# Block inverses of the delta-rule lane: 16x16 diagonal blocks on GpSimd through DRAM, four chunks side by side, levels in kept columns only

## The reference, cut to what matters

```
h = x                                   # (512, 2048)
proj = h @ w_in                         # 4 x 1024 columns + 128 for the delta rule, 4 x 1024 for the gated one
# delta rule (RWKV-7), 16 heads of 64, state S (64 x 64) per head, over t:
sa = S @ a_t
S  = S * w_t + outer(sa, b_t) + outer(v_t, k_t)
o_t = S @ r_t
# gated linear attention (HGRN-2), 8 heads of 128, in chunks:
att[t,s] = (q_t * exp(b_t - b_s)) . k_s   for s <= t
y = concat(o_rwkv, o_hgrn) @ w_out ; h = layer_norm(alpha * x + y)
```

## Time and profile before

| | |
|---|---|
| median of 3 runs | 3407.63 us (3407.55 to 3409.55) |
| the profiled execution: its own time, its span | 3406.94 us, 3405.2 us |
| PE busy | 3214.7 us, 94% |
| VectorE, ScalarE busy | 1726.9 us (51%), 1216.3 us (36%) |
| GpSimd busy | 71.5 us (2%), DMA issues nearly all |
| third block on PE | from about 1680 us to the end |

### The profile page before, as it was taken

One profiled execution on the slowest core, in us unless ns is written; L12 is line 12 of the kernel. 1 busy time (PEld: TensorE's weight loads), 2 busy tenths in 40 slices (PEclk: granted clock), 3 DMA queues, 4 the chain that ended last, 5 costly groups with the idle time before them and its releaser, 6 DMA issues.

```text
span 3405.2 us, 41072 instructions
## 1 busy us (share of the span) xinstructions
PE 3214.7 (94%) x16498; PEld 2578.3 (76%) x16498; DVE 1726.9 (51%) x2865; ACT 1216.3 (36%) x2150; POOL 71.5 (2%) x132
## 2 busy tenths in 40 slices
PE   7999999999999999999999999898999898989896
PEld 5777777777778877777788787777777787877685
DVE  5444444444433355555533546465665555555544
ACT  4333333333323233433333334343434343434421
POOL 0000000000000000000000000000000000000200
PEclk9999999999999999999999999999999999999998
DMA  4222222222233322122243211121211111111532
GB/s 150 75 81 75 75 81 75 76 77 78 68 125 129 106 69 70 67 69 69 98 142 118 68 54 59 44 69 40 70 52 57 56 59 54 63 53 53 192 130 87
DMA packets 79915, 274.86 MB, mean 81 GB/s; under 512 B 9952, under 2 KB 10592, under 8 KB 78960
## 3 DMA queue, kind: packets, MB, share of 16 engines
q1 hardware_dynamic: 63936, 232.13, 20.2%
q0 software_dynamic: 15792, 40.11, 3.5%
HBM read 252.21 MB, written 19.92 MB: 80 GB/s over the span
## 4 chain that ended last, share of the span: by engine, by line
PE 82%; DVE 11%; ACT 3%; issue 3%; DMA 0%; SPq 0%; DVEq 0%; POOL 0%; ACTq 0%
PE bank L253 13%; PE bank L255 13%; PE bank L254 13%; PE bank L257 7%; PE bank L259 7%; PE bank L258 7%; PE bank L1145 2%; PE bank L1152 2%; PE bank L277 2%; PE bank L429 1%; PE bank L1213 1%; PE bank L1159 1%; DVE mc L1082 1%; PE bank L306 1%; PE bank L456 1%
## 5 line engine op out<-in xcount | busy, mean ns | idle before, releaser
L253 PE MATMUL bank<-ma_split,mc_split 128*128 128x512 f32 x2304 | 976.1, 424 | 39.2 <-DVE ma_split L805 18.8
L255 PE MATMUL bank<-ma_split,mc_split 128*128 128x512 f32 x2304 | 908.9, 394 | 0.0
L254 PE MATMUL bank<-ma_split,mc_split 128*128 128x512 f32 x2304 | 905.3, 393 | 0.0
L670 DVE TENSOR_TENSOR mc_split<-mc,mc_split 128x1024 fp32r<-128x1024 f32 x426 | 519.8, 1222 | 428.8 <-ACT mc_split L519 423.9
L519 ACT ACTIVATE mc_split<-mc 128x1024 fp32r<-128x1024 f32 x426 | 448.3, 1054 | 297.7 <-PE bank L257 252.9
L253 PEld LDWEIGHTS bank<-ma_split,mc_split 128*128 128x128 f32 x2304 | 438.3, 190 | 147.7 <-issue 51.8
L255 PEld LDWEIGHTS bank<-ma_split,mc_split 128*128 128x128 f32 x2304 | 435.7, 189 | 97.8
L254 PEld LDWEIGHTS bank<-ma_split,mc_split 128*128 128x128 f32 x2304 | 439.0, 191 | 71.0 <-issue 3.8
L1325 ACT ACTIVATE mc<-bank 128x512 f32<-128x512 f32 x192 | 114.6, 597 | 391.5 <-PE bank L1159 269.1
L528 ACT ACTIVATE mc<-bank,stat 128x128 f32<-128x128 f32 (+3 forms) x128 | 67.6, 528 | 511.4 <-DVE stat L678 511.1
L257 PE MATMUL bank<-mc_split,ma_split 128*128 128x512 f32 x576 | 230.2, 400 | 5.1 <-DMA ma_split<-y 5.0
(11 more groups left out here) (353 smaller groups left out, 4030.4 us busy)
## 6 DMA issues: line engine op xcount, KB each, us to landing
mc<-in_w SPq DMA_DIRECT2D x426, 512.0 KB, 3.2
x<-mc POOLq DMA_DIRECT2D x8, 1024.0 KB, 5.0
y<-mb_split POOLq DMA_DIRECT2D x28, 256.0 KB, 2.8
ma_split<-y POOLq DMA_DIRECT2D x28, 256.0 KB, 7.6
mb<-in_xt SPq DMA_DIRECT2D x8, 512.0 KB, 12.4
mc<-in_x POOLq DMA_DIRECT2D x4, 1024.0 KB, 6.3
mc<-x POOLq DMA_DIRECT2D x4, 1024.0 KB, 5.9
mb<-x POOLq DMA_DIRECT2D x4, 1024.0 KB, 9.8
```

What stands on the lines that cost most here:

```text
L253: mm = pe.matmul(banks[j][:], wh[:, c], act_hi[:, kt, :], start=(kt == 0), stop=False)
L254: pe.matmul(banks[j][:], wl[:, c], act_hi[:, kt, :], start=False, stop=False)
L255: last = pe.matmul(banks[j][:], wh[:, c], act_lo[:, kt, :], start=False, stop=(kt == KT - 1))
L670: dve.tensor_tensor(w_low[:, s % NR, :, :], w_raw[:, s % NR, :, :], w_high[:, s % NH, :, :].bitcast(F32), ALU.subtract).then_inc(w_lo, 1)
```

## The change

1. `m8`, `xt`, `xw` hold eight matrices (two heads, four chunks), so a unit goes through the chunk part once, in 24 steps. `xw` takes the place of `xx` and `wsb`. Room is made by NH = 3 high buffers in place of 4.
2. The 16x16 diagonal blocks of all eight inverses (64 blocks) are made by GpSimd: `m8` is stored to DRAM, its diagonal blocks are loaded with one block on each of 64 partitions, 15 steps of a multiply and an add make the inverses, they are stored, and the 128x128 matrices that hold them are loaded back into `xt`. PE waits for that load (`xt_in`) ahead of its first X.
3. Only levels 4, 5 and 6 are left on PE, VectorE and ScalarE. A W or T matmul has 64 moving columns (those that the level keeps) in place of 128, and so has the copy behind it; the seven levels of the gated branch too.
4. Steps stand further apart: the four G steps (step 9 to 12 of the unit) every 3 points, then 37 points between the last G and the first X, levels every 3 points, the steps behind them every 2.5.

```diff
-NR, NH, LEAD = 5, 4, 2
+NR, NH, LEAD = 5, 3, 2
...
-                if k < 59:
-                    return 120 * u + 28 + 2 * (k - 9)
-                return 120 * u + 128 + 3 * (k - 59)
+                begin = 120 * u + 28
+                i = k - 9
+                if i < 4:
+                    return begin + 3 * i
+                if i < 13:
+                    return begin + 46 + 3 * (i - 4)
+                if i < CHUNK_K:
+                    return begin + 73 + 5 * (i - 13) // 2
+                return begin + 102 + 3 * (i - CHUNK_K)
...
+            def halves(x, lv):
+                v = x.rearrange("p q (n x t) -> p q n x t", x=2, t=1 << lv)
+                return v[:, :, :, 0, :], v[:, :, :, 1, :]
...
+                elif i < 13:
+                    lv, part = FIRST_LEVEL + (i - 4) // 3, (i - 4) % 3
+                    for p in range(2):
+                        mats = range(4 * p, 4 * p + 4)
+                        if part == 0:
+                            if lv == FIRST_LEVEL:
+                                pe.wait_ge(xt_in, 16 * (u + 1))
...
+                            for q in mats:
+                                mm = pe.transpose(C_BANK[f"X{lv}{p}"][:, q % 4 * P:(q % 4 + 1) * P], xt[:, q, :], ident[:])
+                        elif part == 1:
+                            c_wait(pe, "act", u, f"X{lv}{p}")
+                            to = halves(four(C_BANK[f"W{lv}{p}"][:]), lv)[0]
+                            for q in mats:
+                                mm = pe.matmul(to[:, q % 4], m8[:, q, 0:P], halves(xw, lv)[0][:, q], start=True, stop=True)
...
+            def sub_inverses(pool, u):
...
+                c_wait(pool, "dve", u, f"G{2 * NCH - 1}")
+                pool.dma_start(mats(a["mats"]), m8[:, :, 0:P]).then_inc(a_out, 16)
+                pool.wait_ge(a_out, 16 * (u + 1))
+                pool.dma_start(ub, blocks(a["mats"])).then_inc(ub_in, 16)
...
+                pool.memset(yb, 0.0).then_inc(inv_step, 1)
...
+                pool.wait_ge(ub_in, 16 * (u + 1))
+                for k in range(SUB - 1):
+                    size = [2 * NCH * SUBS, k + 1, SUB - 1 - k]
+                    pool.wait_ge(inv_step, n + 2 * k + 2)
+                    pool.tensor_tensor(yt[:, 0:k + 1, k + 1:SUB], yb[:, 0:k + 1, k:k + 1].broadcast_to(size),
+                                       ub[:, k:k + 1, k + 1:SUB].broadcast_to(size), ALU.mult).then_inc(inv_step, 1)
+                    pool.wait_ge(inv_step, n + 2 * k + 3)
+                    pool.tensor_tensor(yb[:, 0:k + 1, k + 1:SUB], yb[:, 0:k + 1, k + 1:SUB], yt[:, 0:k + 1, k + 1:SUB],
+                                       ALU.add).then_inc(inv_step, 1)
+                pool.wait_ge(inv_step, n + 2 * SUB)
+                pool.dma_start(blocks(a["inv"]), yb).then_inc(yb_out, 16)
+                pool.wait_ge(yb_out, 16 * (u + 1))
+                c_wait(pool, "pe", u - 1, f"U{NCH - 1}")
+                pool.dma_start(xt, mats(a["inv"])).then_inc(xt_in, 16)
+                pool.wait_ge(xt_in, 16 * (u + 1))
...
+                              + [(rw_at(u, 13), 2, u) for u in range(UNITS)])
```

More of the change, by code:

```diff
@@ L30 @@
 LEVELS = 7
+SUB = 16
+SUBS = CH // SUB
+FIRST_LEVEL = 4
+MAT_STRIDE = SUBS * (SUB * CH + SUB)
 RANK = 64
@@ L974, in programs @@
             ln_at = rc_.at
-            m4 = rc_(4, 4 * P)
-            xx, xt, wsb = rc_(4, P), rc_(4, P), rc_(4, P)
+            m8, xt, xw = rc_(2 * NCH, 4 * P), rc_(2 * NCH, P), rc_(2 * NCH, P)
+            ub, yb, yt = [rc_(SUB, SUB)[0:2 * NCH * SUBS] for _ in range(3)]
             r0s, us, stbd, stmp = rc_(P), rc_(P), rc_(P), rc_(P)
@@ L1056, in d_out @@
                 eng.wait_ge(d_free, D_BEFORE[key] + D_USES[key[0], key[2]])
[L1059 to L1065, removed]
+            CHUNK = [(f"G{q}", 4 + q % 2, "dve") for q in range(2 * NCH)]
+            for lv in range(FIRST_LEVEL, LEVELS):
+                for what, eng in (("X", "act"), ("W", "act"), ("T", "dve")):
+                    CHUNK += [(f"{what}{lv}{p}", 4 + p, eng) for p in range(2)]
+                    if (what, lv) == ("W", LEVELS - 1):
+                        CHUNK += [("R0", 6, "act")]
+            for c in range(NCH):
+                CHUNK += [(f"R{c}", 6, "act")] * (c > 0) + [(f"U{c}", 4, "dve"), (f"O{c}", 5, "act"), (f"S{c}", 6, "dve")]
             C_BANK = {name: banks[b] for name, b, _ in CHUNK if b}
@@ L1135, in chunk_pe @@
                             hs = slice(h * HD, (h + 1) * HD)
-                            mm = pe.matmul(C_BANK[f"G{h}"][:, 2 * P * half:2 * P * (half + 1)], x[hs, tk],
-                                           ar[hs, c, :, :].rearrange("p x t -> p (x t)"), start=True, stop=True)
+                            mm = pe.matmul(C_BANK[f"G{2 * i + h}"][:, 2 * P * half:2 * P * (half + 1)], x[hs, tk],
+                                           ar[hs, i, :, :].rearrange("p x t -> p (x t)"), start=True, stop=True)
@@ new lines, in chunk_pe @@
+                elif i < 13:
[5 more added lines that the diff above has]
+                                pe.wait_ge(xt_in, 16 * (u + 1))
+                                c_wait(pe, "dve", u, f"G{2 * NCH - 1}")
+                            else:
+                                c_wait(pe, "dve", u, f"T{lv - 1}{p}")
+                            for q in mats:
[5 more added lines that the diff above has]
+                                mm = pe.matmul(to[:, q % 4], m8[:, q, 0:P], halves(xw, lv)[0][:, q], start=True, stop=True)
+                        else:
+                            c_wait(pe, "act", u, f"W{lv}{p}")
+                            to = halves(four(C_BANK[f"T{lv}{p}"][:]), lv)[1]
+                            for q in mats:
+                                mm = pe.matmul(to[:, q % 4], xw[:, q, :], halves(xt, lv)[1][:, q], start=True, stop=True)
+                        mm.then_inc(c_pe, 1)
+                    if i == 11:
+                        chunk_r(pe, u, 0)
+                elif i % 3 == 1:
+                    c = (i - 13) // 3
+                    c_wait(pe, "dve", u, f"T{LEVELS - 1}{c // 2}")
+                    c_wait(pe, "act", u, f"R{c}")
@@ L1210, in hg_pe @@
                     lhs, rhs = (mix[lv % 2], mix[lv % 2]) if lv < LEVELS else (hk, hqs)
+                    to, frm = four(D_BANK[:]), four(rhs)
+                    if lv < LEVELS:
+                        to, frm = halves(to, lv)[1], halves(frm, lv)[1]
                     for c in range(NCH):
-                        tk = slice(c * P, (c + 1) * P)
-                        mm = pe.matmul(D_BANK[:, tk], lhs[:, tk], rhs[:, tk], start=True, stop=True)
+                        mm = pe.matmul(to[:, c], lhs[:, c * P:(c + 1) * P], frm[:, c], start=True, stop=True)
                     mm.then_inc(d_done, 1)
@@ new lines, in chunk_dve @@
+            def chunk_dve(dve, st, u, i):
+                if i < 4:
+                    if u == i == 0:
+                        dve.wait_ge(inv_zeroed, 16)
+                    for q in (2 * i, 2 * i + 1):
+                        c_wait(dve, "pe", u, f"G{q}")
+                        keep_where(dve, m8[:, q, :], tril4[:], C_BANK[f"G{q}"][:]).then_inc(c_dve, 1)
+                elif i < 13:
+                    lv = FIRST_LEVEL + (i - 4) // 3
+                    for p in range(2) if i % 3 == 0 else ():
+                        c_wait(dve, "pe", u, f"T{lv}{p}")
+                        keep_where(dve, halves(xt[:, 4 * p:4 * p + 4, :], lv)[1], level_mask(lv),
+                                   halves(four(C_BANK[f"T{lv}{p}"][:]), lv)[1]).then_inc(c_dve, 1)
+                elif i % 3 == 1:
+                    c = (i - 13) // 3
+                    c_wait(dve, "pe", u, f"U{c}")
+                    dve.tensor_copy(us, C_BANK[f"U{c}"][:, 0:P]).then_inc(c_dve, 1)
+                elif i % 3 == 2:
+                    c = (i - 13) // 3
+                    c_wait(dve, "pe", u, f"S{c}")
+                    st(dve.tensor_tensor(stmp, stbd, C_BANK[f"S{c}"][:, 0:P], ALU.add))
```

217 lines of the change are left out of this document (99 added, 118 removed).

## The result

The changed kernel takes **3349.52 us** (median; 3348.36 to 3353.34), the kernel before took 3407.77 beside it: a ratio of 0.9832, 95% interval 0.9819 to 0.9844. It is 58 us faster where I forecast 91.5; the time lies inside the stated range of 3290 to 3350, by half a microsecond.

The account below looks back on a forecast made before the run. PE, busy 94% of the span, was taken to bound the kernel: -107.5 (levels), -32 (waits), +38 (GpSimd chain), +5 (clock) and +5 (NH = 3) make -91.5 us against 3406.9, so 3316 us, range 3290 to 3350.

Parts of the forecast that it names:

- The forecast case: Whole kernel: PE waits 15 to 70 us in all for the chain, 3316 us; given 45%.
- Chain late: Rival, PE at each unit's first X: chain of 37 to 42 us loses part of the gain, 3385 us; 16%.
- Taken off PE: W, T and X groups on PE: three double levels replace twelve groups of each per unit, -107.5 us over eight units.
- Half the columns: W, T and gated-branch matmuls on PE: 64 columns cost 0.225 us each, like 128, so nothing is gained.
- Both column rivals: Halved matmuls on PE: cheaper by up to 68 us, 3250 us (4%), or strided writes cost 68 us, 3383 us (5%).
- Waits inside the levels: PE's idle time at X, W and T, mostly behind VectorE: 10 of 41.6 us left, -32 us.
- The GpSimd chain: PE before each unit's first X: 33 us from G3 through GpSimd and DMA against 30.5 us of cover, +38 us.
- Unit 0: PE's first chain wait: 5.5 us without a gated branch beside it, plus 4.5 for an ISA instruction, 10 us.
- The clock: PE behind long waits in units 0 and 7: clock at half, some 2.3 us lost each, +5 us.
- Unit 7's store first: GpSimd's sorted list: a gated-branch entry precedes unit 7's chain, which starts 8 us late, so unit 7 waits 11 us.
- NH = 3: One high buffer fewer: ScalarE's and VectorE's splits stand ahead of a slot's steps, +5 us (bounds 0 and 20).

Follow-up runs that it names:

- the seven-level kernel: Changed kernel with all seven levels on TensorE and no inverse work on GpSimd, keeping side by side order, kept columns and three buffers: 3397.68 us, ratio 0.9969.

## Why the prediction held, and where it was off

The forecast case came in, direction and mechanism, but at the very edge of its range (3290 to 3350), and that it stayed inside by half a microsecond is luck: the chain of 37.0 us is as near to the 40 at which the rival *Chain late* was priced as to the forecast's 33, and the waits for the load came out 31 us too long, nearly all of the 33 by which the gain fell short. Taken by its steps:

- **Taken off PE, -107.5 us.** Right. A level costs what I had worked out, 4.46 us for eight matrices, and 24 of them are 107 us.
- **Half the columns, nothing.** Right, shown twice: a pass of 64 columns starts 0.11 us after the last, and whole columns change the time by 0.9 us. Both column rivals (4% and 5%) are out.
- **Waits inside the levels, -32 us.** 41.6 to 3.8, so -38; the seven-level kernel took 34 off as a whole. Right that the order side by side does most of it: with seven levels it leaves 13.7 of the 48.2 us of the kernel before with three buffers, and three levels leave 3.8. Not foreseen: the waits of the gated products and of the turns (L1248, L1119) rise by 14 us.
- **The GpSimd chain, +38 us.** This is the step that failed in size: **+69.0**. The chain was mis-sized by 2 to 5.5 us a unit, the cover by up to 2. With the wait at 2.5 us of a 33 us chain, each of these goes straight into the wait. By the trace, the mean of units 0 to 5 is 37.0 us for 33: the 30 operations and the gaps between them 15.3 for 12, the handovers between engines and queues 1.9 for 1, transfers and masked copies as forecast (the medians of the four transfers make 16.9 us of the 17.3). The operation itself was sized well, 0.28 us undisturbed for 0.30. What was short are two terms: VectorE's share of the memory, 4.9 us a chain where I had 3, and the 0.08 us between dependent operations, 2.3 us a chain, for which I had nothing but a part of the 1 us of semaphores. Leaving the operations out (-81 us) shows that the waits hang on the chain's length, not which of its terms was short.
- **Unit 0, 10 us.** 12.0, near by luck: the 4.5 us for the instruction ahead of the first operation were not seen (it starts 0.07 us after its blocks landed), and the longer chain took their place.
- **The clock, +5 us.** The sum is about right by accident, and not by units 0 and 7 alone. The chain's waits cost 16 us of half clock, as the kernel without the operations shows. Against that, the kernel before lost 11 us in its own level groups (W, T and X took 201 us there from 1850 us on, 11 over 96 times the 0.81 + 0.81 + 0.36 of the earlier trace rows) and 19.9 in slow starts of the stream; the changed one loses 7 and 29.5 there (108.4 us in groups that take 101.3 undisturbed), so 6 us more.
- **Unit 7's store first.** Seen rightly as a delay (GpSimd's first issue 7.7 us after G3's start, where units 0 to 5 have 3.0 to 3.3 and unit 6 4.5), and missed that this order is what the gated take needs.
- **NH = 3, +5 us.** Too low: 22 us on the kernel before, 13 in the changed one. The step had the mechanism in words (both splits ahead of the slot's steps) and its bounds held the 13, not the 22.

Worked from the two traces, from 1850 us on: -107.5 by the levels, +41.6 by all waits (112.4 to 154.0), 2 us by which the third block's first product starts later (1900.99 for 1899.02), some +6 net of clock: -58, against 58.3 between the spans. The third buffer has no term of its own here, since what it costs is in the waits and in the later start.

## What to carry over

A chain that is hidden behind a fixed number of steps has a cliff: once it is as long as its cover, each microsecond that it gains is paid once per unit in waiting and here a quarter more in clock, so size its pieces by measurement and give it slack first (12 points of slack were worth 58 us, as much as the change). When work joins a queue, list who waits for what already stands in it, since 4 us saved at the head cost 27 us at the tail. A buffer removed to make room is a change of its own, to be timed alone, even where the stream that it feeds never waits.

## What the hardware showed beyond the forecast

- Small operations of GpSimd with two inputs (64 x 15 to 64 x 64 elements) took 0.20 to 0.33 us while VectorE stood still, 0.28 in the mean, 0.08 us apart when dependent; memsets of the same outputs 0.15 us. Only the first kind was held up by VectorE, by 4.9 us in 30 operations.
- A transfer cut into 1024 pieces costs GpSimd 0.84 to 0.92 us to issue, where the 256 KB stores cost it 0.55. The 64 KB ones land in 3.1 to 3.9 us, not much sooner than those of 512 KB (4.6 and 5.3).
- A masked copy of half the columns, 128 x 256, lasts as long as a whole one of 128 x 512 (0.73 and 0.74 us) when it takes single columns or pairs (levels 0 and 1 of the gated branch); from runs of four columns on it takes 0.42 to 0.52. Levels 1 and 2 of one unit:

```profile
2250.91 0.73 DVE L1112 COPY_PREDICATED mb<-lmaskt,bank 128x256 f32<-128x256 uint8 x1
2253.24 0.45 DVE L1112 COPY_PREDICATED mb<-lmaskt,bank 128x256 f32<-128x256 uint8 x1
```
